# A Mamba/HGRN trunk with 16 experts on one NeuronCore: finishing the tokens of the last two expert blocks by slot

## What is computed

```python
def reference(x, ...):                       # x: (1, 512, 1024) float32
    h = rmsnorm(x, norm_mix_w)
    proj = h @ w_in                          # 1024 x 3592
    ...                                      # two mixers: Mamba-2 SSD and HGRN2
    x = x + concatenate([y_ssd, y_hgrn]) @ w_out
    h = rmsnorm(x, norm_ffn_w)
    x = x + hier_moe(h, router_group, router_expert, w_gate, w_up, w_down)
    return rmsnorm(x, final_norm_w)

def hier_moe(h, ...):                        # 4 groups of 4 experts, expert width 256
    p_group = softmax(t @ router_group); g_idx, g_w = argmax(p_group), max(p_group)
    in_group = logits of the 4 experts of that group
    top_w, top_i = top_k(softmax(in_group), 2); top_w = top_w / sum(top_w)
    combine = one_hot(expert) * (g_w * top_w)
    y = sum over e of combine[:, e] * ((silu(t @ wg[e]) * (t @ wu[e])) @ wd[e])
```

## Time and profile before

| | us |
|---|---|
| median of 3 runs | 470.52 (470.41 to 471.61) |
| the profiled execution | 473.07 |
| its span, first to last instruction | 471.3 |
| PE busy | 434.8 (92%) |
| DVE busy | 345.0 (73%) |
| ACT busy | 274.1 (58%) |
| POOL busy | 159.9 (34%) |

### The profile page before, as it was taken

One profiled execution on the slowest core, in us unless ns is written; L12 is line 12 of the kernel. 1 busy time (PEld: TensorE's weight loads), 2 busy tenths in 40 slices (PEclk: granted clock), 3 DMA queues, 4 the chain that ended last, 5 costly groups with the idle time before them and its releaser, 6 DMA issues.

```text
span 471.3 us, 7023 instructions
## 1 busy us (share of the span) xinstructions
PE 434.8 (92%) x2707; PEld 380.0 (81%) x2707; DVE 345.0 (73%) x527; ACT 274.1 (58%) x454; POOL 159.9 (34%) x120
## 2 busy tenths in 40 slices
PE   8999999999999899999999987999999999999800
PEld 7678887899998798999999977888888888887600
DVE  4466999756767989899765367577887788767846
ACT  6753555236463172337254344589998999879523
POOL 4660000000013001115200404288878887885210
PEclk9999999999999999999999987999999999999965
DMA  8850224140202134041389412979999999998265
GB/s 306 343 221 31 88 90 136 67 156 6 86 0 91 43 109 147 17 196 72 130 334 359 170 47 73 340 277 369 382 365 349 382 374 370 357 327 321 81 213 203
DMA packets 21055, 94.55 MB, mean 201 GB/s; under 512 B 4844, under 2 KB 7064, under 8 KB 12696
## 3 DMA queue, kind: packets, MB, share of 16 engines
q1 hardware_dynamic: 14280, 83.53, 47.0%
q0 software_dynamic: 4096, 8.41, 5.5%
q10 hardware_dynamic: 2640, 2.11, 1.4%
HBM read 88.79 MB, written 11.54 MB: 213 GB/s over the span
## 4 chain that ended last, share of the span: by engine, by line
PE 58%; DVE 22%; DMA 9%; ACT 7%; issue 3%; POOLq 0%; SPq 0%; DVEq 0%; ACTq 0%
PE bank L1667 31%; DMA arena<-in_w_gate_up_dram 5%; PE bank L2003 4%; PE bank L2005 4%; PE bank L2004 4%; DVE arena L1169 3%; PE bank L1991 2%; PE bank L1743 2%; DVE wl L1090 2%; PE bank L1868 2%; ACT wh L760 1%; DMA pairs_dram<-arena 1%; DVE actl L1549 1%; DMA X<-h_dram,arena 1%; DMA arena<-in_x_first_dram 1%
## 5 line engine op out<-in xcount | busy, mean ns | idle before, releaser
L1667 PE MATMUL bank<-wh,acth 128*128 128x256 f32 x320 | 91.9, 287 | 0.8 <-DVE actl L1084 0.8
L1667 PE MATMUL bank<-wh,actl 128*128 128x256 f32 x320 | 90.5, 283 | 0.0
L1667 PE MATMUL bank<-wl,acth 128*128 128x256 f32 x320 | 90.5, 283 | 0.0
L1667 PEld LDWEIGHTS bank<-wh,acth 128*128 128x128 f32 x320 | 61.2, 191 | 1.1 <-issue 1.0
L625 POOL TENSOR_TENSOR wl<-raw,wh 128x2048 fp32r<-128x2048 f32 x4 | 20.2, 5040 | 121.7 <-ACT wh L760 121.7
L1667 PEld LDWEIGHTS bank<-wl,acth 128*128 128x128 f32 x320 | 61.3, 191 | 0.0
L1667 PEld LDWEIGHTS bank<-wh,actl 128*128 128x128 f32 x320 | 61.2, 191 | 0.0
L704 POOL TENSOR_TENSOR wl<-raw,wh 128x1024 fp32r<-128x1024 f32 x15 | 36.0, 2419 | 44.3 <-ACT wh L955 44.3
L2003 PE MATMUL bank<-wh,acth 128*128 128x512 f32 x124 | 50.1, 404 | 0.6 <-DVE wl L1543 0.4
L2005 PE MATMUL bank<-wh,actl 128*128 128x512 f32 x124 | 48.6, 392 | 0.0
L2004 PE MATMUL bank<-wl,acth 128*128 128x512 f32 x124 | 48.4, 390 | 0.0
(11 more groups left out here) (364 smaller groups left out, 1019.4 us busy)
## 6 DMA issues: line engine op xcount, KB each, us to landing
arena<-in_w_gate_up_dram SPq DMA_DIRECT2D x18, 1024.0 KB, 15.7
raw<-in_w_units_dram SPq DMA_DIRECT2D x17, 1024.0 KB, 4.8
arena<-in_w_down_dram SPq DMA_DIRECT2D x16, 1024.0 KB, 14.1
raw<-in_w_gate_up_dram SPq DMA_DIRECT2D x14, 1024.0 KB, 15.9
arena<-pairs_dram SPq DMA_DIRECT2D x6, 512.0 KB, 5.6
arena<-in_x_first_dram SPq DMA_DIRECT2D x3, 768.0 KB, 7.9
arena<-in_x_dram SPq DMA_DIRECT2D x4, 512.0 KB, 12.6
arena<-in_x_dram SPq DMA_DIRECT2D x1, 2048.0 KB, 11.1
```

The source lines that it names most:

```text
L1667: ins = te.matmul(acc_ap, a, b, start=(j == 0), stop=(j == n - 1))
```

## The change

The weights of a slot are computed once, early: `slot_gates` (DVE) makes each token's two weights in three bfloat16 pieces, 24 more small matmuls in `find_targets` bring them into slot order, and `targets` writes them to `gsl`. ACT multiplies by `gsl` when it moves a result out of PSUM, so rows of `pairs_dram` are weighed already. `find_targets` now comes after the transposes of block 1. The fillers are 44 after `find_all` and 8 after the transposes of block 0, in place of 8, 4 and 4. On DVE `split_c` of block 0, second half, comes after `rest_tokens` of block 1, and the four small steps of `row_lists` come before `targets`; the small steps of `gates` at the end go.

The result is now made of six pieces, in the order of `finished`: the slots of block 14, tile 0, the slots of block 15, tiles 1, 2 and 3. The tokens of blocks 14 and 15 are finished in slot order: POOL gathers their residuals (`own_residuals`, after block 12), adds their first rows by an accumulating gather (`own_first_rows`, before the scatter of block 13), DVE adds `ysb` itself, and the finished rows are scattered to the output. All other tokens are finished by tile: after the scatter of block 13 POOL adds the first rows to `xres` with an accumulating transfer (`add_first`) and gathers the second rows (`second`). The scatters of blocks 14 and 15 are gone. All stores of the result are indirect and issued by POOL (`store_finished`). The residuals also go to DRAM (`keep_rows`), and x is copied to `pairs_dram` in DRAM, before the MoE part. The branch `later_rounds` comes after the finish, behind the six pieces on POOL, ACT, DVE and SP. Some semaphores are merged.

```diff
+        LAST = NE - 2
+        finished = [("slots", 0), ("tile", 0), ("slots", 1), ("tile", 1), ("tile", 2), ("tile", 3)]
+        OUTS = len(finished)
...
@@ -520,6 +535,7 @@
                     split_by(sp, u - RAW)
                 sp.dma_start(raw[:, u % RAW, :], front_src(u)).then_inc(raw_in[u % RAW], 16)
             sp.wait_ge(hg_ev, TT)
+            sp.dma_start(pairs_dram[T:2 * T, :], x[0]).then_inc(xr_st, 16)
             sp.dma_start(xres, x[0].rearrange("(t p) n -> p t n", p=P)).then_inc(xres_in, 16)
...
+            sp.wait_ge(ev_dve, evacuated(n_in_groups + halves_out.index((n_front - 2, 1)))[1])
+            keep_rows(slice(0, units[n_front - 1][1]))
+            sp.wait_ge(h2_st, 16 * (n_front - n_in + 1))
+            keep_rows(slice(units[n_front - 1][1], D))
             sp.wait_ge(gat_in[0], 16)
             load_a(3)
...
+            sp.wait_ge(rows_out, OUTS * 16)
+            later_rounds(sp, sp_round, rows_again, all_rows)
...
                     .then_inc(sca_out[j], 16)
+
+            def slots_of(e):
+                return bass.IndirectOffsetOnAxis(ap=gix[0:CAP, PERM[e]:PERM[e] + 1], axis=0)
+
+            def own_residuals():
+                pool.wait_ge(xr_st, 48)
+                wait_a(pool, 0, LAST - 1)
+                pool.sem_inc(pool_tick, 1)
+                for i in range(2):
+                    gp.indirect_dma_start(own_rows[i][0:CAP, :], None, xres_dram, slots_of(LAST + i),
+                                          bounds_check=T - 1, oob_is_err=False).then_inc(own_in, 16)
+
+            def own_first_rows():
+                for j in range(YB):
+                    pool.wait_ge(sca_out[j], (NE - G) // YB * 16)
+                pool.wait_ge(own_in, 32)
+                pool.sem_inc(pool_tick, 1)
+                for i in range(2):
+                    gp.indirect_dma_start(own_rows[i][0:CAP, :], None, pairs_dram[0:T, :], slots_of(LAST + i),
+                                          bounds_check=T - 1, oob_is_err=False, compute_op=ALU.add)\
+                        .then_inc(own_in, 16)
+
+            def add_first(tt):
+                gp.dma_start(xres[:, tt, :], pairs_dram[tt * P:(tt + 1) * P, :], accum_op=ALU.add).then_inc(first_in[tt], 16)
+
+            def second(tt):
+                gp.indirect_dma_start(late[tt], None, pairs_dram,
+                                      bass.IndirectOffsetOnAxis(ap=rix[:, TT + tt:TT + tt + 1], axis=0),
+                                      bounds_check=2 * T - 1, oob_is_err=False).then_inc(gat_in[tt], 16)
+
+            def store_finished(n):
+                kind, i = finished[n]
+                pool.wait_ge(fin_ok, n + 1)
+                pool.sem_inc(pool_tick, 1)
+                if kind == "slots":
+                    gp.indirect_dma_start(out[0], slots_of(LAST + i), own_rows[i][0:CAP, :], None, bounds_check=T - 1,
+                                          oob_is_err=False).then_inc(rows_out, 16)
+                else:
+                    gp.indirect_dma_start(out[0], bass.IndirectOffsetOnAxis(ap=rix[:, i:i + 1], axis=0), late[i], None,
+                                          bounds_check=T - 1, oob_is_err=False).then_inc(rows_out, 16)
...
+                    if first_round and e >= LAST:
+                        continue
+                    if first_round and e == LAST - 1:
+                        own_first_rows()
                     scatter(r, base, e)
+                    if first_round and e == LAST - 2:
+                        own_residuals()
...
             pool_round(0, 0, True)
-            later_rounds(pool, pool_round)
+            add_first(0)
+            add_first(1)
+            for j in range(YB):
+                pool.wait_ge(sca_out[j], LAST // YB * 16)
+            pool.sem_inc(pool_tick, 1)
+            second(0)
+            second(1)
+            for tt in range(2, TT):
+                add_first(tt)
+                second(tt)
+            for n in range(OUTS):
+                store_finished(n)
+            later_rounds(pool, pool_round, last_scatters, add_again)
...
+                if e == 0:
+                    act.wait_ge(six_ok, 2 * r + 2)
                 act.wait_ge(dn, step * 2 + 3)
                 y_free(act, r, e, first_round)
-                sc.activation(ysb[e % YB][:, 0:512], bank[5][:, :], ACT.Copy).then_inc(y0_ok, 1)
+                weight = gsl[:, PERM[e]:PERM[e] + 1]
+                sc.activation(ysb[e % YB][:, 0:512], bank[5][:, :], ACT.Copy, scale=weight).then_inc(y0_ok, 1)
                 act.wait_ge(dn, step * 2 + 4)
-                sc.activation(ysb[e % YB][:, 512:1024], bank[6][:, :], ACT.Copy).then_inc(y1_ok, 1)
+                sc.activation(ysb[e % YB][:, 512:1024], bank[6][:, :], ACT.Copy, scale=weight).then_inc(y1_ok, 1)
...
+            def slot_gates():
+                dve.wait_ge(ge_ok, 1)
+                ch.link(ve.tensor_reduce(r1[:, 6], r4[:, 1], AX_X, ALU.add))
+                dve.wait_ge(e2_ok, 1)
+                ch.link(ve.scalar_tensor_tensor(r1[:, 7], r1[:, 4], 1.0, r1[:, 6], ALU.add, ALU.mult))
+                ch.link(ve.reciprocal(r1[:, 8], r1[:, 7]))
+                ch.link(ve.tensor_tensor(r1[:, 9], r1[:, 8], r1[:, 4], ALU.mult))
+                gv = r16[:, 4:6]
+                ch.link(ve.tensor_tensor(gv, r16[:, 1:3], r1[:, 8:10].unsqueeze(3).broadcast_to([P, 2, TT, NE]),
+                                         ALU.mult))
+                for i in range(2):
+                    ch.link(ve.tensor_copy(gvp[:, i], gv))
+                    ch.link(ve.tensor_tensor(gv, gv, gvp[:, i], ALU.subtract))
+                ve.tensor_copy(gvp[:, 2], gv).then_inc(gt_v, 1)
+
+            def row_lists():
+                ch.link(ve.tensor_tensor(r1[:, 13], mb[:, :, PERM[LAST]], mb[:, :, PERM[LAST + 1]], ALU.add))
+                ch.link(ve.tensor_scalar(r1[:, 14], r1[:, 13], float(4 * T), float(NO_SLOT), ALU.mult, ALU.add))
+                ch.link(ve.tensor_tensor(r1[:, 15:17], tokc.rearrange("p t i -> p i t"),
+                                         r1[:, 14:15].broadcast_to([P, 2, TT]), ALU.add))
+                ch.link(ve.tensor_copy(rix.rearrange("p (i t) -> p i t", i=2), r1[:, 15:17]))
+
...
                 split_b(base, 0, 0)
                 split_b(base, 0, 1)
+                if first_round:
+                    slot_gates()
+                rest_tokens(base, 0)
                 split_c(base, 0, 0)
-                rest_tokens(base, 0)
+                rest_tokens(base + 1, 1)
                 split_c(base, 0, 1)
-                rest_tokens(base + 1, 1)
                 c = slice(UNIT // 2, UNIT)
                 dve.wait_ge(wha_ok, (base + 1) * 2 + 2)
                 ve.tensor_tensor(wl[:, 0, c], raw_a[1][:, c], wh[:, 0, c].bitcast(F32), ALU.subtract).then_inc(wl1_ok, 1)
                 if first_round:
-                    targets(0)
+                    row_lists()
+                targets(r)
                 hidden(base, 0)
                 split_b(base + 1, 1, 0)
                 split_b(base + 1, 1, 1)
+                if first_round:
+                    count_rounds()
...
+            def add_second(tt):
+                ve.tensor_tensor(late[tt], late[tt], xres[:, tt, :], ALU.add).then_inc(res_ok, 1)
+
+            def final_add(n):
+                kind, i = finished[n]
+                if kind == "tile":
+                    dve.wait_ge(first_in[i], 16)
+                    dve.wait_ge(gat_in[i], (NE // HGB + 1) * 16)
+                    add_second(i)
+                else:
+                    dve.wait_ge(own_in, 64)
+                    dve.wait_ge(y0_ok, LAST + i + 2)
+                    dve.wait_ge(y1_ok, LAST + i + 2)
+                    ve.tensor_tensor(own_rows[i], ysb[(LAST + i) % YB], own_rows[i], ALU.add).then_inc(res_ok, 1)
+
+            def final_norm(n, rows_of, column):
+                dve.wait_ge(fsd_ok, n + 1)
+                ch.link(ve.reciprocal(st[:, 1, column:column + 1], st[:, 5, column:column + 1]))
+                ve.scalar_tensor_tensor(rows_of, rows_of, st[:, 1, column:column + 1], bc[:, :], ALU.mult,
                                         ALU.mult).then_inc(fin_ok, 1)
...
+            final_add(0)
+            for n in range(1, OUTS):
+                final_add(n)
+                final_norm(n - 1, final_rows(n - 1), n - 1)
+            final_norm(OUTS - 1, final_rows(OUTS - 1), OUTS - 1)
+            later_rounds(dve, dve_round, None, finish_again)
...
+                        te.matmul(bank[7][:, NE:2 * NE], onehot[:, c, tt, :], vals6[:, c, tt],
+                                  start=(c == 0 and tt == 0), stop=(c == 1 and tt == TT - 1))
+                pe.wait_ge(gt_v, 1)
+                for c in range(2):
+                    for tt in range(TT):
+                        for i in range(3):
+                            ins = te.matmul(bank[7][:, 2 * NE:3 * NE], onehot_b[:, c, tt, :], gvp[:, i, c, tt],
+                                            start=(c == 0 and tt == 0 and i == 0),
```

(13 more changed lines are left out.)

185 lines of the change are left out of this document (88 added, 97 removed).

## The result

The changed kernel takes 490.56 us (median of 4 runs, 489.73 to 492.2) against 470.7 of the kernel before on the same chip: 1.0423 times as long, 95% interval 1.0392 to 1.0453. The sign was right, the size was not: +19.9 us instead of +10.3, above the upper end of the range. The profiled execution took 492.2, its span is 490.5 against 471.3. The last matmul of a block starts at 456.24 against 447.03, so 9.2 us are lost ahead of it (forecast 6.0, and 0.6 within the term of the end); from there to the end of the span it is 34.2 us against 24.3, so 9.9 more (forecast 4.3 less these 0.6).

What follows compares the result with a forecast made beforehand. The prediction took PE to bound the middle, with transfers close behind. It added 6.0 us at the start and 4.3 at the end to the profiled 473.07, giving 483.4 profiled and 480.8 as median; range 472.5 to 486.5.

Steps and rivals of the forecast that it cites:

- Start of the blocks, +6.0: Ahead of the first blocks: fillers in PE's path cost 3.8 us, DVE's lengthened chain behind block 1's transposes 2.2.
- The other early parts: nothing.: Early part: scale on ACT's copy, slot_gates, copy of x and stores of residuals were all taken to cost 0.
- Is it hidden later? No.: Middle blocks: bound by PE, with weights loaded as buffers come free, so the 6 us late start stays.
- the wait of 2.29 stays: Block 14: ACT's wait of 2.29 us for weights was to remain, since the weights come 6 us later too.
- rival C: Middle: transfers, not PE, set it, so the 6 us vanish and the time is 468; chance 0.10.
- PE in blocks 14 and 15, +0.6: Block 15: POOL's split_a ends 2.2 us later, PE regains most, leaving +0.6 on the last product.
- The end, +4.3: After the middle: POOL's chain of transfers, DVE's pieces, last store and SP's branch cost +4.5, 0.2 of it counted with PE.
- rival D: Early DRAM copy of x takes more than its 13.4 us slack, up to 490; 0.08 together with a still slower end.
- Profiled against median: Whole kernel: the median was taken to stand 2.55 us below the profiled execution, turning 483.4 into 480.8.
- both upper ends of the sum (7.4 and 9): Highest values given for the two terms: start 7.4 with fillers of 0.27 us, end +9 with slower POOL transfers.
- D or a still slower end: Last of four cases: copy of x beyond its slack, or an end slower than forecast; chance 0.08.

Runs made afterwards that it cites:

- e4: Kernel before with only PE's new order and fillers (44, then 8; find_targets' products behind block 1's transposes): 474.76 us against 471.0.
- e12: Kernel before's end with the changed kernel's head: 44 fillers, gates by slot, count_rounds behind block 1's split, no row_lists: 478.93 us.
- e9: Kernel before with PE's new order and fillers, but 26 fillers instead of 44: no difference, 0.998 to 1.0016 times the kernel before.
- e1: Changed kernel with count_rounds moved back ahead of slot_gates on DVE: 3.3 us less by the median than the changed kernel's 490.56.
- e3: Changed kernel with count_rounds ahead of slot_gates and 26 fillers instead of 44: 483.48 us.
- e15: e5 with the four tile pieces stored by SP's queue, the slot pieces still scattered by POOL: 478.66 us.
- e16: e15 with the accumulation also taken off all six transfers (own_first_rows and add_first): 473.42 us.
- e5: e3 with the scatter of block 13 ahead of the two own_first_rows on POOL: 480.32 us.
- e8: e3 with another end: scatter 13 first, add_first and second during blocks 14 and 15, own_first_rows last, tiles finished first, SP's branch early: 478.37 us.
- e7: e3 with SP reading the count and branching before it waits for the last stores: 2.1 us less than 483.5.
- e11: e3 with the scatter of block 13 ahead of own_first_rows and SP's branch ahead of its last wait: 480.32 us.
- e10: Kernel before's end with 26 fillers, gates by slot and the changed kernel's DVE order, count_rounds ahead of slot_gates, no row_lists: 471.73 us.
- e14: e3 with the accumulation taken off the four add_first alone: 478.63 us.
- e2: Changed kernel with 26 fillers instead of 44 ahead of block 0's transposes, nothing else: 484.59 us.

## Why the prediction was right and wrong

**Start of the blocks, +6.0.** Right: fillers to 296.25 (296.4), block 1's transposes 301.70 (301.9), the chain of DVE 5.5 late at 311.44 (6.0), with the clock at 1.00 up to there. All of the start makes 9.6 us at the transposes of block 3: 4.4 at those of block 2, 1.1 for the chain of DVE, 2.5 for the steps of the next paragraph and 1.6 for the clock.

**"The other early parts: nothing."** This step failed by what it left out. `count_rounds` is moved too, from DVE's wait for the table to a place beneath POOL's split, and the text does not name it. Four steps of one column looked like nothing; they took 5.0 us on a chain that I had myself called without slack. It was not asked beside what they land, and the neighbour on the other engine was not looked at. 4.1 us at block 3, of which 1.6 came by the clock behind PE's wait. The bound that the prediction gave to small steps of `row_lists`, no more than the 0.68 of 512 columns, does not hold for a step beside POOL's split: one of a single column took 2.36.

**"Is it hidden later? No."** It held, as far as the runs show. By the medians 3.8 us arrive of a start that was 2.75 late at block 15 (e4), 7.7 of 7.1 (e12), and against e9 the last products are as late as the transposes of block 15. That "the wait of 2.29 stays" was wrong: it is 0.38 in the changed kernel. But the wait comes and goes between executions, is absent in e9, which starts earlier, and is there in e1, e3, e15 and e16, so it is no sign of rival C.

**PE in blocks 14 and 15, +0.6.** From the transposes of block 15 to the last product the undisturbed versions with the old end take 18.0 (e9, e12), those with the new end 19.0 to 19.1 (e5 to e8): +1.0.

**The end, +4.3.** This step failed by two landings. The chain was the right one, step by step, and its prices were too low. Measured on the clock of the forecast (9.2 taken off): the residuals are there at 441.6 instead of 439; the scatter of block 13 is issued at 445.95 instead of 442.8, and lands at 454.0 instead of 447.5, 8.1 us after its issue where I took 4.7 from the last scatter of the kernel before; tile 0 starts on DVE at 459.7 instead of 452.9; the chain of DVE from there took 14.4, not 15.3; the end is 481.3 instead of 475.8. The failed terms are these two landings. The residuals were taken to land 8 us after their issue, with 10.6 as the upper end, and took about 12 (438.70 to 450.79). The scatter's 4.7 was taken from a transfer that was alone in its queue. That an accumulating transfer might be slower than a copy was not bounded at all, though no row has one. In the forecast tile 0 started on DVE 4.8 us sooner behind the last product than before, and this paid for the longer chain and the longer last hop; measured it is 2.6 later. DVE's chain and the last hop came out 1.3 below their prices together. The rule of the Trainium skill that I had weighed ("DMA: Bandwidth & Descriptors", "Anatomy of one DMA — SWDGE (gpsimd) path") gives 3.1 us for such a transfer and says nothing of what accumulation costs; it is further from the 8.1 than the row was. SP's branch, priced at 1.7, costs nothing as long as POOL's drain ends 2.0 us behind the last landing (e7, e11), so that the sum of the two last hops was about right by luck (7.2 us from DVE's last scaling to the end, forecast 7.6).

**The copy of x (rival D).** The load of x landed 15.6 us after its issue instead of 11.1, and no wait of DVE came of it; right.

**Profiled against median.** I took 2.55 us off; the changed kernel's profiled execution stands 1.64 above its median. That is 0.9 of the miss of 9.8. Of the rest 3.2 lie ahead of the last product (9.2 against 6.0) and 5.6 behind it (9.9 against 4.3); with the 0.6 that the prediction put into the second term but ahead of the last product, 2.6 and 6.2. The 2.55 were not a constant: the profiled execution of the kernel before had its wait for weights, from the transposes of block 15 to the last product it took 19.9 us where e9 and e12 take 18.0.

**The range.** With both upper ends of the sum (7.4 and 9) the time is 486.9, about the top of the range. The result lies 3.7 beyond: 9.2 and 9.9 were measured for the two. The ends bounded the size of terms that I had, and nothing stood for a term that I had not seen. Of the four cases it is the last, "D or a still slower end", given 0.08; rival D itself did not come about.

## What to carry to other kernels

A step that is moved is priced by its new neighbours, not by its size: ask which instruction of POOL runs beside each small DVE step with two inputs in SBUF. Before work is moved to POOL's queue, add up the whole queue, transfer by transfer, with the accumulating ones at a price of their own, and ask what POOL still has to drain when the program ends. And when the head and the end of a kernel are changed together, build the head with the old end first: here (e10) it shows no loss, and nearly all of the rest is the end.

No version beats the kernel before by more than a measurement can tell: e9, with 26 fillers, has a span of 468.0 in its profile and the same time by the medians.

## What the runs showed of the hardware

- A DVE instruction of one column with two inputs in SBUF lasts 2.3 to 2.4 us, instead of 0.16, beside an instruction of POOL's split, and one of POOL's 3.0 instead of 2.4 behind one of DVE's split; by the records they take turns for whole instructions.
- Six transfers of 448 or 512 KB that add to their target cost 6.1 us over plain ones, about 1 each (2.1 for two and 4.9 for four, each with the noise of a single step); the direct ones land 9.2 instead of 6.5 us after their issue. Their issue costs POOL more too. The groups of that line in the changed kernel and in e14 (busy us, mean ns):
```profile
L753 POOL DMA_DIRECT2D arena<-pairs_dram x4 | 3.8, 1053 | 0.0
```
```profile
L753 POOL DMA_DIRECT2D arena<-pairs_dram x4 | 2.4, 598 | 0.0
```
- POOL's drain at the end of the program ends 2.0 us behind the landing of its last transfer in the eleven versions whose stores are all POOL's, and then ends the span. In the other seven it ends 1.4 to 1.9 behind it and other work ends later.
- After the same wait of 2.22 us, between the same matmuls, PE's granted clock fell to 0.50 from 318 to 321 in the changed kernel and stayed at 1.00 in e2 and e12.
